# Differential scores of a two-layer encoder: two products with rows moved by transfers in place of three

## The chip, the cores and the metric

The kernel runs on one core of a Trainium2 chip. The metric is the device time of one execution, in microseconds (us). The core has a matrix engine (TensorE, PE in the profile, its weight loads PEld), VectorE (DVE), ScalarE (ACT), GpSimd (POOL) and SyncE (SP). SP issues nearly all transfers of this kernel. Results of TensorE go to eight banks of 128 x 512 fp32.

## What is computed

A trunk of two layers is applied, with the same weights, to two requests of 512 positions by 1024 features. Each layer has an attention part and a feed-forward part. The attention part has four heads of differential attention and four of latent attention. Cut to the first kind:

```
q, k = rope(h @ w_q), rope(h @ w_k)              # per head two components c of 64 features
sc   = einsum('bqhcd,bkhcd->bhcqk', q, k) * 64 ** -0.5
p    = softmax(sc)
a    = p[:, :, 0] - lam * p[:, :, 1]
o    = a @ v                                     # then rms norm, output projection, residual
```

All is fp32. The kernel splits an fp32 operand into a high part, rounded to fp32r, and a low part, the difference. A product of two operands is made as high x high + high x low + low x high, three matmuls into one bank.

## The kernel before

The program goes through layer 0 and layer 1; in each it does the attention of request 0, the attention of request 1 (the document calls these four stretches halves, numbered in order of time), and then the feed-forward part of both requests.

In a half each engine follows an order written out by hand: `TENSOR_ORDER` (L71), `SCALAR_ORDER` (L83) and `VECTOR_ORDER` (L94). Semaphores connect them; an engine that waits holds everything behind it in its order. The steps that matter here:

- TensorE: `P q0` is the projection of the two components of head 0's q to one bank (24 matmuls of 512 columns); `Pa` and `Pb` are its first and second half where it is cut in two. `S i` are the scores of unit i. Units 0 to 15 are differential: unit i is head i // 4 and a block of 128 queries, i mod 4, and has two scores, one for each component c. `T i` transposes the combined probabilities, `A` multiplies them with the values, `ST` and `RB` belong to norms.
- ScalarE: `RH` writes the high part of a roped tile (L1437, `rope_his`), `EX i` the exponentials of unit i, `TH` the high part of the transposed probabilities (L1485).
- VectorE: `RP` applies the rotary tables from the bank into the tile r1 (L1904, `rope`), `RL` makes the low part (L1920, `rope_los`), `MX` the maxima of a unit, `CB` combines the two components, `TL` makes the low part of the transposed probabilities.

TensorE begins a half's heads with `P q0 | P k0 | P q1 | S 0 | Pa k1 | S 1 | Pb k1 | T 0 | S 2 | Pa q2 | S 3 | T 1 | Pb q2 | Pa k2 | S 4`. So the first score of head 0 stands behind the projection of q1, and that of head 1 is unit 4. ScalarE has `EX 0 | EX 1 | RH q1 | TH 0 | EX 2 | TH 1 | RH k1 | EX 3 | TH 2`, VectorE `RL q1 | MX 2 | TL 0 | RP k1 | CB 2 | RL k1 | MX 3`.

A q tile has 128 rows: 32 of component 0, 32 of component 1, then the second halves of both again. `qd[n][c]` holds q's high and low part for component c: the rows of the other component are zero, since the copy multiplies with a mask (L1447, L1934). `kd[n]` holds the high and the low part of both components. n is the head mod 2, so a tile is written again two heads later. A score is the three matmuls of `product` (L526): q high by k high (L528), q high by k low (L529), q low by k high (L530), with 128 query columns as weights and 512 key columns moving. Half the rows of q add nothing to it.

The weights of a chunk (1 MB with both parts) are loaded by SP from memory as TensorE frees one of three slots (L619). In the first half ScalarE and POOL make the two parts from the raw weights (L1519, L853) and SP stores them.

Of the kernel before, what the change touches and what calls it, by code (L numbers as in the profile page):

```python
# [9 lines left out]
ACT = mybir.ActivationFunctionType  # L10
F32 = mybir.dt.float32
F32R = mybir.dt.float32r
# [3 lines left out]
P = 128  # L16
D = 1024
KT = D // P
T = 512
NT = T // P  # L20
L = 2
B = 2
H = 4
# [43 lines left out]
def order(text):  # L67
# [13 lines left out]
    ob5 | P ob6 | P ob7  # L81
""")
SCALAR_ORDER = order("""  # L83
    V | RH q0 | RH k0 | EX 0 | EX 1 | RH q1 | TH 0 | EX 2 | TH 1 | RH k1 | EX 3 | TH 2 | EX 4 | RH q2 | EX 5 | TH 3 |
    YC 0 | TH 4 | RH k2 | EX 6 | RH q3 | TH 5 | EX 7 | TH 6 | EX 8 | RH k3 | TH 7 | EX 9 | EX 10 | SH y0 | TH 8 |
    YC 1 | TH 9 | EX 11 | LC ckv | TH 10 | EX 12 | RH kpe | SH y1 | TH 11 | EX 13 | EX 14 | SH ckv | LC cq0 | LC cq1 |
    TH 12 | EX 15 | TH 13 | SH cq | YC 2 | PH kn0 | TH 14 | PH qn0 | TH 15 | RH pe0 | EX 16 | PH vm0 | PH vm1 |
    PH vm2 | YC 3 | PH vm3 | PH kn1 | SH y2 | EX 17 | TH 16 | PH qn1 | EX 18 | EX 19 | SQ 0 | PH kn2 | SQ 1 | TH 17 |
    SH y3 | EX 20 | SQ 2 | TH 18 | PH qn2 | RH pe1 | PH kn3 | EX 21 | TH 19 | PH qn3 | EX 22 | EX 23 | EX 24 | TH 20 |
    YC 4 | EX 25 | EX 26 | TH 21 | TH 22 | EX 27 | TH 23 | TH 24 | SQ 3 | SQ 4 | YC 5 | TH 25 | EX 28 | TH 26 |  # L90
    EX 29 | EX 30 | SQ 5 | SQ 6 | TH 27 | SQ 7 | SN 0 | TH 28 | SN 1 | SN 2 | TH 29 | EX 31 | SN 3 | SN 4 | SN 5 |
    TH 30 | YC 6 | TH 31 | YC 7 | SN 6 | SN 7
""")
VECTOR_ORDER = order("""  # L94
    V | RP q0 | RL q0 | RP k0 | RL k0 | RP q1 | MX 0 | MX 1 | CB 0 | CB 1 | RL q1 | MX 2 | TL 0 | RP k1 | CB 2 |
# [37 lines left out]
def numbered(names):  # L133
    return {n: i for i, n in enumerate(names)}
# [2 lines left out]

DV_MM = 7
ROPED = numbered([s[1] for s in VECTOR_ORDER if s[0] == "RP"])
ROPE_SPLITS = numbered([(n, c) for n in ROPED for c in range(2 if n[0] in "qp" else 1)])  # L140
PLAIN = numbered(["dv0", "dv1", "dv2", "dv3"] + [s[1] for s in VECTOR_ORDER if s[0] == "PL"])
LATENT = numbered([s[1] for s in SCALAR_ORDER if s[0] == "LC"])
OUTS = numbered([s[1] for s in VECTOR_ORDER if s[0] == "XO"])
# [127 lines left out]
def encoder_trunk(nc, xT, watt, wffn, tables, gains, lam, out):  # L271
    with ExitStack() as ctx:
        KB = 1024
# [7 lines left out]
        def at(name, shape, offset, dt=F32):  # L281
            return nc.alloc_sbuf_tensor_at(name, shape, dt, offset=offset)

        def psum(name):
# [53 lines left out]
        p_hi, p_lo = [ppair[:, i, :] for i in range(2)]  # L338
        qd = [[[at(f"qd{n}{c}_{s}", [P, T], r_qk + (n * 12 + c * 4 + i * 2) * KB, F32R)
                for i, s in enumerate(("hi", "lo"))] for c in range(2)] for n in range(2)]  # L340
        kd = [[at(f"kd{n}_{s}", [P, T], r_qk + (n * 12 + 8 + i * 2) * KB, F32R)
               for i, s in enumerate(("hi", "lo"))] for n in range(2)]

        cq = [[at(f"cq{n}_{s}", [P, T], r_qk + (n * 4 + i * 2) * KB, F32R)
               for i, s in enumerate(("hi", "lo"))] for n in range(2)]
# [62 lines left out]
        def sem(name):  # L408
            return ctx.enter_context(nc.semaphore(name))
# [46 lines left out]
        s_roped = Count(sem("roped"), len(ROPED))  # L456
        s_rope_hi = Count(sem("rope_hi"), len(ROPE_SPLITS))
        s_rope_lo = Count(sem("rope_lo"), len(ROPE_SPLITS))
        s_latent = Count(sem("latent_copied"), len(LATENT))
        s_xo = Count(sem("output_added"), len(OUTS))  # L460
        s_score = Count(sem("scores_done"), NEV)
# [70 lines left out]
        def stacked_product(pe, out_ap, lhs, rhs, first):  # L532

            nc.tensor.matmul(out_ap, lhs, rhs[0], start=first, stop=False)  # L534
            return nc.tensor.matmul(out_ap, lhs, rhs[1], start=False, stop=True)  # L535

        def rope_target(name):

            if name == "kpe":
                return [kpe], None  # L540
            n = int(name[-1])
            if name[0] == "p":
                return [qpe[2 * n], qpe[2 * n + 1]], 2
            return (qd[n % 2], 0) if name[0] == "q" else ([kd[n % 2]], None)

        def plain_target(name):
            n = int(name[2])
# [456 lines left out]
        def _(pe):  # L1004
# [135 lines left out]
            def scores(l, b, i):  # L1140
                h, qt = i // NT, i % NT
                at_q = slice(qt * P, (qt + 1) * P)
                for c in range(2 if i < 16 else 1):
                    ev = 2 * i + c if i < 16 else 32 + i - 16
                    dst = bank[2 + ev % 3][:]

                    pe.wait_ge(s_exp.sem, s_exp.half_at(l, b, ev - 3))
                    if ev < 3:

                        pe.wait_ge(s_plain_lo.sem, s_plain_lo.half_at(l, b, PLAIN[f"dv{ev}"]))  # L1150
                    if i < 16:
                        if qt == 0:

                            pe.wait_ge(s_rope_lo.sem, s_rope_lo.half_at(l, b, max(ROPE_SPLITS[(f"k{h}", 0)], ROPE_SPLITS[(f"q{h}", 1)])))
                        last = product(pe, dst, [qd[h % 2][c][s][:, at_q] for s in range(2)],
                                       [kd[h % 2][s][:] for s in range(2)], True, True)
                    else:
                        h -= H
                        if qt == 0:
                            pe.wait_ge(s_plain_lo.sem, s_plain_lo.half_at(l, b, max(PLAIN[f"qn{h}"], PLAIN[f"kn{h}"])))  # L1160
                            pe.wait_ge(s_rope_lo.sem, s_rope_lo.half_at(l, b, max(ROPE_SPLITS[(f"pe{h // 2}", h % 2)],
                                                                                 ROPE_SPLITS[("kpe", 0)])))
                        product(pe, dst, [qn[h % 2][s][:, at_q] for s in range(2)], [kn[h % 2][s][:] for s in range(2)],
                                True, False)
                        last = stacked_product(pe, dst, qpe[h][:, at_q], [kpe[s][:] for s in range(2)], False)
                    last.then_inc(s_score.sem, 1)
# [220 lines left out]
        def _(act):  # L1387
# [49 lines left out]
            def rope_his(l, b, name):  # L1437
                dst, scale = rope_target(name)
                act.wait_ge(s_roped.sem, s_roped.half_at(l, b, ROPED[name]))
                if name[0] == "p":  # L1440
                    act.wait_ge(s_mm.sem, s_mm.half_at(l, b, DV_MM + LAST_Z))
                elif name == "kpe":
                    act.wait_ge(s_score.sem, s_score.half_at(l, b, 23))
                elif int(name[1]) > 1:
                    act.wait_ge(s_score.sem, s_score.half_at(l, b, 8 * int(name[1]) - 9))
                for c, d in enumerate(dst):
                    nc.scalar.activation((d if name[0] == "p" else d[0])[:], r1[:], ACT.Copy, scale=1.0 if scale is None else  # L1447
                                         masks[:, scale + c:scale + c + 1]).then_inc(s_rope_hi.sem, 1)

            def latent_copy(l, b, name):  # L1450

# [90 lines left out]
            for l in range(L):  # L1542
                for b in range(B):
                    for step in SCALAR_ORDER:
                        kind, what = step[0], step[-1]
                        if l == 0 and b == 0:
                            for j in FIRST_ROUNDS.get(" ".join(str(word) for word in step), []):
                                slot_hi(j)
                        if kind == "V":
                            if b == 0:  # L1550
                                act.wait_ge(s_dg.sem, s_dg.layer_at(l, 0))
                            else:
                                act.wait_ge(s_dg.sem, s_dg.half_at(l, 0, STATS.index("n")))
                            for m in range(NT):

                                act.wait_ge(s_mm.sem, s_mm.half_at(l, b, 3 + m))
                                nc.scalar.activation(v[0][:, m, :], bank[2 + m][:], ACT.Copy,
                                                     scale=rstd[:, m:m + 1]).then_inc(s_plain_hi.sem, 1)
                        elif kind == "RH":
                            rope_his(l, b, what)  # L1560
                        elif kind == "LC":
                            latent_copy(l, b, what)
                        elif kind == "PH":
                            plain_hi(l, b, what)
                        elif kind == "EX":
                            exponentials(l, b, what)
                        elif kind == "TH":
                            transposed_hi(l, b, what)
                        elif kind == "YC":
                            head_out(l, b, what)  # L1570
                        elif kind == "SH":
                            normed_hi(l, b, what)
                        elif kind == "SQ":
                            norm_square("tail", l, b, what)
                        elif kind == "SN":
                            x_hi("tail", l, b, what)
# [226 lines left out]
        def _(dve):  # L1803
# [116 lines left out]
            def rope_los(l, b, name):  # L1920
                q0 = min(n for (tn, c), n in ROPE_SPLITS.items() if tn == name)
                dst, scale = rope_target(name)
                for c, d in enumerate(dst):
                    dve.wait_ge(s_rope_hi.sem, s_rope_hi.half_at(l, b, q0 + c))
                    if name[0] == "p":
# [554 lines left out]
```

## Time and profile before

| | |
|---|---|
| median of 3 runs | 2270.39 us (2268.04 to 2270.62) |
| profiled execution | 2269.12 us |
| its span | 2267.3 us |
| mean granted clock of TensorE | 0.997 |
| PE busy | 2232.9 us, 98% |
| DVE busy | 1803.7 us, 80% |
| ACT busy | 984.7 us, 43% |
| POOL busy | 990.3 us, 44% |
| TensorE matmuls | 10610 |

How to read it: the shares are means over the whole span, attention and feed-forward together. The granted clock is given as a share of full speed (1.00 is 2.4 GHz, 0.50 is 1.2 GHz). The duration of a matmul is longer than the distance to the next one, since matmuls overlap. The four halves lie at about 0 to 240, 240 to 490, 1115 to 1360 and 1360 to 1600 us. The profiled execution's own time is 1.8 us above its span.

### The profile page before, as it was taken

The numbers are of one execution on the slowest core, as the hardware profiler recorded it, in microseconds if no ns is written. First come the engines' busy times: TensorE is split into PE (matmuls) and PEld (weight loads), VectorE is DVE, ScalarE is ACT, GpSimd is POOL, SyncE is SP. The second block draws the span as 40 slices with busy tenths as digits, with TensorE's granted clock in tenths as the row PEclk, the third lists the DMA queues.
The fourth block names the chain that finished last, engine by engine and source line by source line (L and its number), as shares of the span: only waits on it lengthen the run. The fifth ranks groups of instructions, "written<-read, shape, count | busy, mean of one in ns | idle before, by whom it ended". The sixth has DMA issues, their size and how long they took to land.

```text
span 2267.3 us, 31231 instructions
## 1 busy us (share of the span) xinstructions
PE 2232.9 (98%) x10610; PEld 1858.7 (82%) x10610; DVE 1803.7 (80%) x2793; ACT 984.7 (43%) x1876; POOL 990.3 (44%) x686
## 2 busy tenths in 40 slices
PE   8999999999999999999999999999999999999998
PEld 6888888888888888888888888888888888888886
DVE  7998388888787878999958873988877676779988
ACT  4556144554444444443324541455444434444342
POOL 4314100124777777798700010001254455568893
PEclk9999999999999999999999999999999999999999
DMA  8633542233676766853243136312323232357522
GB/s 306 221 111 124 205 174 94 83 141 117 215 239 215 236 216 235 316 175 108 99 149 112 56 130 214 121 59 110 135 84 111 97 111 97 111 212 261 165 72 84
DMA packets 93463, 346.89 MB, mean 153 GB/s; under 512 B 9760, under 2 KB 9888, under 8 KB 74016
## 3 DMA queue, kind: packets, MB, share of 16 engines
q1 hardware_dynamic: 92624, 344.53, 43.7%
q8 instruction: 64, 1.05, 0.2%
q10 hardware_dynamic: 720, 0.86, 0.1%
q14 instruction: 55, 0.45, 0.1%
HBM read 237.35 MB, written 108.00 MB: 152 GB/s over the span
## 4 chain that ended last, share of the span: by engine, by line
PE 87%; DVE 6%; issue 1%; ACT 1%; POOL 0%; DVEq 0%; ACTq 0%; POOLq 0%
PE bank L528 28%; PE bank L530 27%; PE bank L529 27%; PE bank L1177 2%; PE bank L1015 1%; DVE x L2234 1%; DVE u L2200 1%; PE bank L1023 1%; PE bank L535 1%; PE bank L534 1%; DVE qpe L1928 1%; DVE aT_lo L2053 1%; DVE y_out L2341 0%; ACT aT_hi L1490 0%; DVE x L2242 0%
## 5 line engine op out<-in xcount | busy, mean ns | idle before, releaser
L905 POOL TENSOR_TENSOR slot<-raw,slot 128x512 fp32r<-128x512 f32 x160 | 223.4, 1400 | 234.4 <-ACT slot L1629 234.4
L528 PE MATMUL bank<-h_hi,slot 128*128 128x512 f32 x640 | 249.2, 389 | 0.0
L529 PE MATMUL bank<-h_lo,slot 128*128 128x512 f32 x640 | 249.1, 389 | 0.0
L530 PE MATMUL bank<-h_hi,slot 128*128 128x512 f32 x640 | 249.1, 389 | 0.0
L882 POOL TENSOR_TENSOR acc<-sq,zero 128x512 f32<-128x512 f32 x5 | 6.1, 1219 | 528.3 <-ACT sq L1418 528.3
L528 PE MATMUL bank<-u,slot 128*128 128x512 f32 x560 | 218.6, 390 | 1.1 <-DVE x L2234 1.1
L529 PE MATMUL bank<-u,slot 128*128 128x512 f32 x560 | 218.1, 389 | 0.0
L530 PE MATMUL bank<-u,slot 128*128 128x512 f32 x560 | 218.0, 389 | 0.0
L528 PE MATMUL bank<-h_hi,w 128*128 128x512 f32 x512 | 203.6, 398 | 0.0
L905 POOL TENSOR_TENSOR slot<-s_stage,slot 128x512 fp32r<-128x512 f32 x120 | 175.8, 1466 | 60.1 <-ACT slot L1629 58.6
L530 PE MATMUL bank<-h_hi,w 128*128 128x512 f32 x512 | 200.0, 391 | 0.0
L529 PE MATMUL bank<-h_lo,w 128*128 128x512 f32 x512 | 199.6, 390 | 0.0
L864 POOL TENSOR_TENSOR w<-raw,w 128x512 fp32r<-128x512 f32 x70 | 101.1, 1466 | 215.2 <-ACT w L1525 111.8
L529 PE MATMUL bank<-t_lo,slot 128*128 128x512 f32 x480 | 186.9, 389 | 0.0
L528 PE MATMUL bank<-t_hi,slot 128*128 128x512 f32 x480 | 186.9, 389 | 0.0
L530 PE MATMUL bank<-t_hi,slot 128*128 128x512 f32 x480 | 186.9, 389 | 0.0
L2234 DVE TENSOR_TENSOR x<-x,bank 128x512 f32<-128x512 f32 x280 | 175.3, 676 | 10.9 <-PE bank L530 10.6
L2200 DVE TENSOR_TENSOR u<-uf,u 128x512 fp32r<-128x512 f32 x140 | 170.5, 1257 | 13.8 <-ACT u L1659 13.8
L1482 ACT ACTIVATE e<-bank,mx 128x512 f32<-128x512 f32 x192 | 130.6, 686 | 99.1 <-DVE mx L2045 99.0
L2156 DVE TENSOR_TENSOR bank<-bank,snap 128x512 f32<-128x512 f32 x80 | 55.7, 696 | 143.7 <-PE bank L530 143.7
L1639 ACT ACTIVATE snap<-bank 128x512 f32<-128x512 f32 x160 | 95.5, 597 | 152.0 <-PE bank L530 151.9
L1629 ACT ACTIVATE slot<-raw 128x512 fp32r<-128x512 f32 x160 | 100.1, 627 | 97.1 <-DVE raw L2145 52.3
(261 smaller groups left out, 5931.6 us busy)
## 6 DMA issues: line engine op xcount, KB each, us to landing
w<-parked SPq DMA_DIRECT2D x81, 1024.0 KB, 4.9
raw<-in_wffn SPq DMA_DIRECT2D x112, 512.0 KB, 3.5
u_kept<-made SPq DMA_DIRECT2D x148, 256.0 KB, 2.8
uf<-u_kept SPq DMA_DIRECT2D x70, 512.0 KB, 5.7
parked<-w SPq DMA_DIRECT2D x27, 1024.0 KB, 6.3
parked<-p SPq DMA_DIRECT2D x27, 1024.0 KB, 4.9
raw<-in_watt SPq DMA_DIRECT2D x27, 512.0 KB, 4.3
praw<-in_watt SPq DMA_DIRECT2D x27, 512.0 KB, 5.8
```

The lines of the kernel that those rows point to most:

```text
L528: nc.tensor.matmul(out_ap, lhs[0], rhs[0], start=first, stop=False, skip_group_check=joins)
L529: nc.tensor.matmul(out_ap, lhs[0], rhs[1], start=False, stop=False, skip_group_check=joins)
L530: return nc.tensor.matmul(out_ap, lhs[1], rhs[0], start=False, stop=last, skip_group_check=joins)
L864: last = nc.gpsimd.tensor_tensor(w[slot][1][:, cols], src[:, cols], w[slot][0][:, cols].bitcast(F32), ALU.subtract)
L905: nc.gpsimd.tensor_tensor(slot[i][:, 1, :], gate_source(i), slot[i][:, 0, :].bitcast(F32), ALU.subtract).then_inc(s_gate_lo.sem, 1)
L1177: last = nc.tensor.transpose(bank[5][:, k * P:(k + 1) * P], src[:, k * P:(k + 1) * P], ident[:])
L1482: nc.scalar.activation(e[e_buffer(ev)][:], bank[2 + ev % 3][:], ACT.Exp, bias=mx[:, ev:ev + 1], accum_out=ls[:, ev:ev + 1]).then_inc(s_exp ...
L1629: nc.scalar.activation(slot[i][:, 0, :], gate_source(i), ACT.Copy).then_inc(s_gate_hi.sem, 1)
L1639: nc.scalar.activation(snap[n][:], bank[4 * (1 - tt) + at][:], ACT.Copy).then_inc(s_snap.sem, 1)
L2156: nc.vector.tensor_tensor(z[:], z[:], snap[2 * b][:], ALU.add).then_inc(s_joined.sem, 1)
L2200: nc.vector.tensor_tensor(upair[d % 2][g][:, q, 1, :], upair_f[d % 2][g][:, q, 1, :], upair[d % 2][g][:, q, 0, :].bitcast(F32), ALU.subtra ...
L2234: nc.vector.tensor_tensor(xn, xn, at[m][:], ALU.subtract if g == N3 else ALU.add).then_inc(s_acc.sem, 1)
```

## The change

A differential score takes two matmuls. The high part of k is written twice, into `kd[n][0]` and `kd[n][1]`; the low part of k goes to a tile of its own, `k_low`. Then small transfers issued by ScalarE put, in `kd[n][c]`, the low rows of component c in the place of the other component's rows, and, in `qd[n][c]` high, a second copy of component c's rows in the place of the zero rows. With that, one product of q high with `kd[n][c]` is high x high + high x low, and the product of q low, whose other rows are still zero, with the same tile is low x high. The step is named `MV` in ScalarE's order. It waits for the low part of its tile (q's low part reads the zero rows, k's low part is what is moved), and issues four transfers, each of 32 rows by 512 elements (64 KB). The first score of a head waits for the transfers' semaphores. `MV` stands in ScalarE's order behind `RH q0`, behind `RH k0`, between `TH 1` and `RH k1` (for q1), behind `EX 3` (k1), behind `TH 4` (q2), behind `EX 6` (k2), behind `TH 6` (q3) and behind `EX 9` (k3). The orders of the other engines are the same.

```diff
 SCALAR_ORDER = order("""
-    V | RH q0 | RH k0 | EX 0 | EX 1 | RH q1 | TH 0 | EX 2 | TH 1 | RH k1 | EX 3 | TH 2 | EX 4 | RH q2 | EX 5 | TH 3 |
+    V | RH q0 | MV q0 | RH k0 | MV k0 | EX 0 | EX 1 | RH q1 | TH 0 | EX 2 | TH 1 | MV q1 | RH k1 | EX 3 | MV k1 |
+    TH 2 | EX 4 | RH q2 | EX 5 | TH 3 | YC 0 | TH 4 | MV q2 | RH k2 | EX 6 | MV k2 | RH q3 | TH 5 | EX 7 | TH 6 |
+    MV q3 | EX 8 | RH k3 | TH 7 | EX 9 | MV k3 | EX 10 | SH y0 | TH 8 | YC 1 | TH 9 | EX 11 | LC ckv | TH 10 | EX 12 |
...
-        kd = [[at(f"kd{n}_{s}", [P, T], r_qk + (n * 12 + 8 + i * 2) * KB, F32R)
-               for i, s in enumerate(("hi", "lo"))] for n in range(2)]
+        kd = [[at(f"kd{n}{c}", [P, T], r_qk + (n * 12 + 8 + c * 2) * KB, F32R) for c in range(2)] for n in range(2)]
+        k_low = at("k_low", [P, T], r_s + 6 * KB, F32R)
...
+        s_q_moved = [sem(f"q_high_rows_doubled{n}") for n in range(2)]
+        s_k_moved = [sem(f"k_low_rows_placed{n}") for n in range(2)]
...
+        def doubled_product(pe, out_ap, lhs, rhs):
+
+            nc.tensor.matmul(out_ap, lhs[0], rhs, start=True, stop=False)
+            return nc.tensor.matmul(out_ap, lhs[1], rhs, start=False, stop=True)
...
+        def moved_value(l, b, h):
+
+            return 4 * 16 * ((l * B + b) * (H // 2) + h // 2 + 1)
+
+        def block_rows(c):
+
+            return [(own, 32 * (own // 32 ^ 1)) for own in (32 * c, 64 + 32 * c)]
...
-                            pe.wait_ge(s_rope_lo.sem, s_rope_lo.half_at(l, b, max(ROPE_SPLITS[(f"k{h}", 0)], ROPE_SPLITS[(f"q{h}", 1)])))
-                        last = product(pe, dst, [qd[h % 2][c][s][:, at_q] for s in range(2)],
-                                       [kd[h % 2][s][:] for s in range(2)], True, True)
+                            pe.wait_ge(s_q_moved[h % 2], moved_value(l, b, h))
+                            pe.wait_ge(s_k_moved[h % 2], moved_value(l, b, h))
+                        last = doubled_product(pe, dst, [qd[h % 2][c][s][:, at_q] for s in range(2)], kd[h % 2][c][:])
...
+            def move_rows(l, b, name):
+
+                n = int(name[1]) % 2
+                act.wait_ge(s_rope_lo.sem, s_rope_lo.half_at(l, b, ROPE_SPLITS[(name, 1)]))
+                for c in range(2):
+                    for own, other in block_rows(c):
+                        if name[0] == "q":
+                            tile_ = qd[n][c][0].bitcast(F32)
+                            act.dma_start(tile_[other:other + 32, :], tile_[own:own + 32, :]).then_inc(s_q_moved[n], 16)
+                        else:
+                            act.dma_start(kd[n][c].bitcast(F32)[other:other + 32, :], k_low.bitcast(F32)[own:own + 32, :]).then_inc(
+                                s_k_moved[n], 16)
...
+                if key_tile(name):
+                    h = int(name[1])
+                    dve.wait_ge(s_rope_hi.sem, s_rope_hi.half_at(l, b, q0 + 1))
+                    if h:
+                        dve.wait_ge(s_k_moved[(h - 1) % 2], moved_value(l, b, h - 1))
+                    nc.vector.tensor_tensor(k_low[:], r1[:], dst[0][:].bitcast(F32), ALU.subtract).then_inc(s_rope_lo.sem, 2)
+                    return
```

## Rows read from the trace of the kernel before

**Rows 1.** The page's busy time, share of the span and instructions.

```profile
PE 2232.9 (98%) x10610; PEld 1858.7 (82%) x10610; DVE 1803.7 (80%) x2793; ACT 984.7 (43%) x1876; POOL 990.3 (44%) x686
```

**Rows 2.** Windows: length, busy time of each engine, granted clock, DMA share, GB/s.

```profile
45.00:60.00 15.00, 14.04 (x62) 11.33 (x61) 12.70 (x21) 7.24 (x18) 5.93 (x4) 1.00 0.75 286
...
140.00:150.00 10.00, 7.77 (x54) 7.32 (x54) 8.90 (x20) 5.38 (x12) 4.52 (x4) 0.86 0.66 247
...
1404.00:1416.00 12.00, 12.00 (x55) 9.94 (x54) 8.80 (x14) 2.49 (x6) 0.00 (x0) 1.00 0.79 285
...
1432.00:1463.00 31.00, 31.00 (x169) 26.48 (x168) 28.05 (x59) 14.48 (x33) 0.00 (x0) 1.00 0.33 111
```

**Rows 3.** The tile of the low keys: duration in ns, first and last start.

```profile
L529 PE MATMUL bank<-kd_lo,qd_hi x128: 386/390/402, 52.1 to 1496.8; 128*128 128x512 f32 x128
```

**Rows 4.** Timeline of PE, fourth half: start, duration, instruction (units 0, 4, 8).

```profile
1410.96 0.39 PE L528 MATMUL bank<-kd_hi,qd_hi 128*128 128x512 f32 x1
...
1411.64 0.39 PE L528 MATMUL bank<-kd_hi,qd_hi 128*128 128x512 f32 x1
...
1430.97 0.39 PE L528 MATMUL bank<-kd_hi,qd_hi 128*128 128x512 f32 x1
...
1455.72 0.39 PE L528 MATMUL bank<-kd_hi,qd_hi 128*128 128x512 f32 x1
```

**Rows 5.** Timeline of VectorE, fourth half.

```profile
1409.24 0.69 DVE L1932 TENSOR_TENSOR kd_lo<-r,kd_hi 128x512 fp32r<-128x512 f32 x1 [0.70 <-ACT kd_hi L1447]
...
1415.92 1.37 DVE L2045 TENSOR_REDUCE mx<-bank 128x1 f32<-128x512 f32 x2 [0.74 <-PE bank L530]
...
1424.67 0.69 DVE L1918 TENSOR_TENSOR r<-r,r 128x512 f32<-128x512 f32 x1
...
1426.84 0.69 DVE L1932 TENSOR_TENSOR kd_lo<-r,kd_hi 128x512 fp32r<-128x512 f32 x1 [0.36 <-ACT kd_hi L1447]
1427.45 1.28 DVE L2045 TENSOR_REDUCE mx<-bank 128x1 f32<-128x512 f32 x2
...
1446.10 0.69 DVE L1932 TENSOR_TENSOR kd_lo<-r,kd_hi 128x512 fp32r<-128x512 f32 x1 [0.41 <-ACT kd_hi L1447]
```

**Rows 6.** Timeline of ScalarE, fourth half.

```profile
1408.57 0.63 ACT L1447 ACTIVATE kd_hi<-r 128x512 fp32r<-128x512 f32 x1 [4.10 <-DVE r L1918]
...
1425.69 0.60 ACT L1490 ACTIVATE aT_hi<-bank 128x512 fp32r<-128x512 f32 x1 [2.77 <-PE bank L1177]
1426.18 0.62 ACT L1447 ACTIVATE kd_hi<-r 128x512 fp32r<-128x512 f32 x1
...
1428.17 0.69 ACT L1482 ACTIVATE e<-bank,mx 128x512 f32<-128x512 f32 x1 [1.36 <-DVE mx L2045]
```

**Rows 7.** Timeline: DMA issues on ScalarE's queue at the kernel's start.

```profile
14.82 0.33 ACTq L1533 DMA_DIRECT2D e<-in_lam  x1
...
15.19 0.48 ACTq L1534 DMA_DIRECT2D cs<-in_tables  x1
```

**Rows 8.** The page's DMA issues: KB each, median us from issue to landing.

```profile
out_yT<-y_out SPq DMA_DIRECT2D x8, 256.0 KB, 2.2
...
g<-in_gains SPq DMA_DIRECT2D x1, 36.0 KB, 1.8
...
ident<-in_tables ACTq DMA_DIRECT2D x1, 64.0 KB, 4.8
```

**Rows 9.** Timelines of VectorE and PE at head 0, first and third half.

```profile
50.65 1.00 DVE L1932 TENSOR_TENSOR kd_lo<-r,kd_hi 128x512 fp32r<-128x512 f32 x1 [0.70 <-ACT kd_hi L1447]
...
51.80 0.47 PE L528 MATMUL bank<-kd_hi,qd_hi 128*128 128x512 f32 x1 [0.96 <-DVE kd_lo L1932]
...
1173.57 0.69 DVE L1932 TENSOR_TENSOR kd_lo<-r,kd_hi 128x512 fp32r<-128x512 f32 x1 [0.70 <-ACT kd_hi L1447]
...
1174.41 0.47 PE L528 MATMUL bank<-kd_hi,qd_hi 128*128 128x512 f32 x1
```

**Rows 10.** Timeline of PE: the wait in the window of lower clock.

```profile
145.58 0.65 PE L1023 MATMUL bank<-ident,yy 128*128 128x128 f32 x4 [2.19 <-DVE yy L1874]
```

More of the change, by code:

```diff
@@ L83 @@
 SCALAR_ORDER = order("""
-    V | RH q0 | RH k0 | EX 0 | EX 1 | RH q1 | TH 0 | EX 2 | TH 1 | RH k1 | EX 3 | TH 2 | EX 4 | RH q2 | EX 5 | TH 3 |
[L85 to L92, printed above, removed]
+    V | RH q0 | MV q0 | RH k0 | MV k0 | EX 0 | EX 1 | RH q1 | TH 0 | EX 2 | TH 1 | MV q1 | RH k1 | EX 3 | MV k1 |
+    TH 2 | EX 4 | RH q2 | EX 5 | TH 3 | YC 0 | TH 4 | MV q2 | RH k2 | EX 6 | MV k2 | RH q3 | TH 5 | EX 7 | TH 6 |
+    MV q3 | EX 8 | RH k3 | TH 7 | EX 9 | MV k3 | EX 10 | SH y0 | TH 8 | YC 1 | TH 9 | EX 11 | LC ckv | TH 10 | EX 12 |
+    RH kpe | SH y1 | TH 11 | EX 13 | EX 14 | SH ckv | LC cq0 | LC cq1 | TH 12 | EX 15 | TH 13 | SH cq | YC 2 |
+    PH kn0 | TH 14 | PH qn0 | TH 15 | RH pe0 | EX 16 | PH vm0 | PH vm1 | PH vm2 | YC 3 | PH vm3 | PH kn1 | SH y2 |
+    EX 17 | TH 16 | PH qn1 | EX 18 | EX 19 | SQ 0 | PH kn2 | SQ 1 | TH 17 | SH y3 | EX 20 | SQ 2 | TH 18 | PH qn2 |
+    RH pe1 | PH kn3 | EX 21 | TH 19 | PH qn3 | EX 22 | EX 23 | EX 24 | TH 20 | YC 4 | EX 25 | EX 26 | TH 21 | TH 22 |
+    EX 27 | TH 23 | TH 24 | SQ 3 | SQ 4 | YC 5 | TH 25 | EX 28 | TH 26 | EX 29 | EX 30 | SQ 5 | SQ 6 | TH 27 | SQ 7 |
+    SN 0 | TH 28 | SN 1 | SN 2 | TH 29 | EX 31 | SN 3 | SN 4 | SN 5 | TH 30 | YC 6 | TH 31 | YC 7 | SN 6 | SN 7
 """)
@@ L139 @@
 ROPED = numbered([s[1] for s in VECTOR_ORDER if s[0] == "RP"])
-ROPE_SPLITS = numbered([(n, c) for n in ROPED for c in range(2 if n[0] in "qp" else 1)])
+ROPE_SPLITS = numbered([(n, c) for n in ROPED for c in range(1 if n == "kpe" else 2)])
 PLAIN = numbered(["dv0", "dv1", "dv2", "dv3"] + [s[1] for s in VECTOR_ORDER if s[0] == "PL"])
@@ L543, in rope_target, with key_tile @@
                 return [qpe[2 * n], qpe[2 * n + 1]], 2
-            return (qd[n % 2], 0) if name[0] == "q" else ([kd[n % 2]], None)
+            return (qd[n % 2], 0) if name[0] == "q" else (kd[n % 2], None)
+        def key_tile(name):
+            return name[0] == "k" and name != "kpe"
+        def moved_value(l, b, h):
+            return 4 * 16 * ((l * B + b) * (H // 2) + h // 2 + 1)
+        def block_rows(c):
+            return [(own, 32 * (own // 32 ^ 1)) for own in (32 * c, 64 + 32 * c)]
         def plain_target(name):
@@ L1446, in rope_his @@
                 for c, d in enumerate(dst):
-                    nc.scalar.activation((d if name[0] == "p" else d[0])[:], r1[:], ACT.Copy, scale=1.0 if scale is None else
+                    nc.scalar.activation((d if name[0] == "p" or key_tile(name) else d[0])[:], r1[:], ACT.Copy, scale=1.0 if scale is None else
                                          masks[:, scale + c:scale + c + 1]).then_inc(s_rope_hi.sem, 1)
+            def move_rows(l, b, name):
[9 more added lines that the diff above has]
+                                s_k_moved[n], 16)
             def latent_copy(l, b, name):
@@ L1560, in _ @@
                             rope_his(l, b, what)
+                        elif kind == "MV":
+                            move_rows(l, b, what)
                         elif kind == "LC":
```

## The prediction

> **What bounds the kernel now.** I read the page's busy shares first: TensorE is busy 2232.9 of 2267.3 us [rows 1], so whatever is taken off it is worth time if nothing else becomes late. Then the table by stretches [rows 2]: in the attention stretch 1432 to 1463 us TensorE has no gap (31.00 of 31), VectorE is busy 28.05 and ScalarE 14.48. So VectorE is only 3 us behind being the bound itself. The third view is the tile of the products with the low keys [rows 3]: 128 of them, the products that go. The attention runs four times (2 layers, 2 requests; "halves" below), so 32 in each. The last views are the timelines of the three engines around the first heads [rows 4 to 6], because there the order of the work leaves the least room between a key tile's last write and its first score.
>
> **What is removed.** Three products of one score take 1411.64 - 1410.96 = 0.68 us start to start [rows 4], so one is worth 0.227 us (its 0.39 us duration overlaps its neighbour's). A unit (two scores) gets 0.454 us shorter, a half 7.26, the kernel **-29.0 us**, all of it on the engine that sets the end.
>
> **What is added.** Per head ScalarE issues four transfers for q and four for k, of 32 rows by 2 KB, 128 in all, and makes one more copy of k. VectorE's low part of k stays one instruction. The 16 more copies (0.63 us each [rows 6]) and the issues lie in ScalarE's idle half [rows 2], except where named below. VectorE's new wait before the low part of k is for the transfers of the head before, about 19 us older (1427.45 to 1446.10 [rows 5]): nothing. SP and POOL get no new step; SP's weight loads follow TensorE's progress, as before. q's transfers are issued ahead of k's and land first.
>
> Price of an issue: ScalarE's queue shows one at 14.82 and the next at 15.19 [rows 7], 0.37 us apart. No row of before has one with 32 rows, so it can be anything from nearly 0 to the 0.48 of the second one; I take 0.37. The Trainium skill, "DMA: Bandwidth & Descriptors", section "Anatomy of one DMA", states about 50 ns of sequencer dispatch for one transfer (on GpSimd's path, not this one); the rows show 0.33 and 0.48 us, and by the page the rival "cheap issue" below would hold.
>
> Price of a landing: none goes SBUF to SBUF in the trace. Small or late transfers of other kinds landed 1.8 us (36 KB) and 2.2 us (256 KB) after their issue, one of 64 KB amid loads took 4.8 [rows 8]. I take 2.0, by the two nearest in quiet, and keep 4.8 as the upper end and 1.8 as the lower.
>
> **First score of head 0.** Before, in the fourth half: k's high part 1408.57 [rows 6], its low part 1409.24 to 1409.93 [rows 5], the first score 1410.96 [rows 4], when the projection of q1 is over. So there is 1.0 us to spare. Now: one more copy (0.63), then four issues (the last starts 3 x 0.37 = 1.1 after the first), then 2.0 to land: 1409.93 + 3.73 = 1413.66, that is 2.7 us late. Second half: the same spacing, 2.7. First half: 51.65 + 3.73 against 51.80, third: 1174.26 + 3.73 against 1174.41 [rows 9], 3.6 each. Sum **+12.6 us**. Behind the waiting score on TensorE stands everything else; the next to be late is VectorE's maximum of the second unit.
>
> **First score of head 1 (unit 4).** I follow the fourth half. With the first score at 1413.66 and shorter units, the second unit ends near 1418.2 in place of 1416.4, and VectorE, which has hardly an idle moment from 1415.92 to 1425.36 [rows 5], is 1.9 us late: k1 is roped at 1427.3. ScalarE reaches its transposed copy (1425.69 before [rows 6]) at 1426.4, and now the four issues for q1 stand between it and k1's copies (1426.18 before): 1427.9. Two copies end at 1429.15, the low part at 1429.9, then the maximum and the two exponentials of unit 3 (before: 1427.45, 1428.17 and 0.68 later) come first in ScalarE's order: the issues for k1 begin at 1431.25, the last starts at 1432.35 and lands at 1434.4. Before, this score began at 1430.97 [rows 4]: 3.4 us late. TensorE alone would be there at +2.7 - 4 x 0.454 = +0.9. So 2.5 us are waited for here, in each half: **+10.0 us**.
>
> Heads 2 and 3 are covered. k2's low part ends at 1446.79 and its first score begins at 1455.72 [rows 4, 5]: 8.9 us. The new chain needs 0.6 + 1.4 (maximum and exponentials) + 1.1 + 2.0 = 5.1, and TensorE comes up to 1.8 closer. With a landing of 4.8 us it would be 0.8 us short.
>
> **VectorE and ScalarE behind TensorE.** After unit 4 VectorE is 3.4 us late and TensorE gets shorter by some 2.7 us until 1463. VectorE has 2.95 us idle in that stretch [rows 2]. What is given back lies between 0 and 2.7 per half; I take 0.75, nearer nothing because the idle time is the larger: **+3.0 us**.
>
> **The clock.** The granted clock is 1.00 (2.4 GHz) nearly everywhere. In 140 to 150 us it is 0.86, around a wait of 2.19 us of TensorE behind a run of short products [rows 2, 10]. A mean of 0.86 between the two levels means 2.8 us at 1.2 GHz, so 1.4 us of work lost. The eight new waits are longer, 2.5 to 3.6 us, but come behind dense products. Bounds: none or all eight of them, 0 to 11.2; I take four, **+5.6 us**. The Trainium skill, "TensorE: Matmul & The Clock Gate", Part 1, says that an idle TensorE falls to 1.2 GHz; the row agrees for one wait, and by the page the rival "clock at every wait" would hold.
>
> **Sum.** -29.0 + 12.6 + 10.0 + 3.0 + 5.6 = +2.2 us. The profiled execution took 2269.12 us for a span of 2267.3 (1.8 us around it), giving 2271.3; the median of the runs is 1.3 above it, so the forecast is 2270.39 + 2.2 = **2272.6 us**. A difference under 0.2% (4.5 us) is about what a measurement of this kernel can't tell from nothing.
>
> **Rivals.**
> - **Slow landing.** The transfers are small but share the DMA engines with weight loads and the store of x: the share is 0.75 at the first score of the first half and 0.79 at that of the fourth [rows 2]. If a landing takes 4.8 us at three first scores and at unit 4 of the first half, 4 x 2.8 = +11.2: 2283.8 us. For it: the row of 4.8. Against: that transfer started with the kernel's first loads. This is the case on the slower side; with the forecast at +2.2, it passes the 4.5 us of no change from about 2.6 us per landing at these four places. Chance 0.22.
> - **Cheap issue.** If an issue costs next to nothing, the first score comes 1.1 us earlier per half, and at unit 4 another 1.5 go (0.5 or more of the hold before k1, about 1.0 at the end): 4 x 2.6 = -10.4, 2262.2 us, and with fewer clock drops down to 2257. It passes -4.5 us from issues of about 0.13 us and less, which save two thirds of it. For it: in the trace the issues on ScalarE's queue run beside its copies. Against: their spacing of 0.37. Chance 0.27.
> - **Clock at every wait.** 8 x 1.4 in place of 5.6: 2278.2 us. For it: the new waits are longer than the one that cost clock. Chance 0.09.
> - **VectorE becomes the bound.** All that TensorE gains to 1463 is given back: 4 x 2.7 in place of 3.0, 2280.4 us. Against: 2.95 us idle there. Chance 0.05.
> - **It is hidden after all.** The transfers land before their scores and the change keeps its 29.0 us: 2241.4 us. Against: 1.0 us to spare at three first scores at best, less than the fastest landing of the trace. Chance 0.04.
>
> **Chances.** The forecast has 0.33. Faster by over 0.2%: most of cheap issue (0.22), all of hidden (0.04) and the forecast's lower tail (0.04), 0.30. Slower: 0.20 of slow landing, 0.06 of the clock, 0.04 of VectorE, 0.06 of the forecast, 0.36. The rest, 0.34, is within. The range, 2259 to 2286 us, reaches over cheap issue and slow landing; outside are the hidden case, and the worst meetings of two of them (every landing 4.8 us would add 22).
>
> **What would show it.** In the new profile: two score products per score, 0.227 us apart; TensorE waiting for a DMA at the first score of head 0 (about 2.7 to 3.6 us) and of head 1 (about 2.5) in each half and nowhere at heads 2 and 3; DMA issues on ScalarE's queue 0.37 us apart and landings of 2.0; windows with a granted clock under 1.00 after some waits. I am wrong if the waits at units 0 and 4 sum to under 12 or over 35 us, or if VectorE is named as releaser for more than a few us.

## The result and the profile after

The changed kernel takes **2332.91 us** (2332.12 to 2334.95, 4 runs) against 2269.22 (2267.76 to 2270.62, 4 runs) for the one before: ratio 1.0282, 95% interval 1.0264 to 1.0300. It is slower by 64 us; the forecast was 2272.6, with a range that ends at 2286. The profiled span is 2333.2 us (before 2267.3), the mean granted clock 0.980 (before 0.997).

The list of waits of TensorE, after:

```profile
engine line waited for: us in total, times, longest us
PE bank L541 <- DMA kd<-k_low: 64.3, 8, 13.4
...
PE bank L541 <- ACT e L1513: 3.5, 6, 1.4
...
PE bank L1195 <- DVE e L2046: 2.0, 4, 0.8
```

Eight waits for a transfer, 64.3 us together: the first score of head 0 and of head 1 in each half, and no others. So the places are those of the forecast, and the sum is nearly three times its 22.6 us. TensorE's timeline at four of them (the first half, then the fourth):

```profile
66.09 0.77 PE L541 MATMUL bank<-kd,qd_hi 128*128 128x512 f32 x1 [13.41 <-DMA kd<-k_low]
...
98.04 0.76 PE L541 MATMUL bank<-kd,qd_hi 128*128 128x512 f32 x1 [10.40 <-DMA kd<-k_low]
...
1473.03 0.77 PE L541 MATMUL bank<-kd,qd_hi 128*128 128x512 f32 x1 [10.70 <-DMA kd<-k_low]
1473.59 0.63 PE L542 MATMUL bank<-kd,qd_lo 128*128 128x512 f32 x1
1474.02 0.63 PE L541 MATMUL bank<-kd,qd_hi 128*128 128x512 f32 x1
...
1497.55 0.77 PE L541 MATMUL bank<-kd,qd_hi 128*128 128x512 f32 x1 [4.24 <-DMA kd<-k_low]
```

Head 0 waits 13.41, 10.56, 6.55 and 10.70 us in the four halves, head 1 10.40, 4.20, 4.22 and 4.24. Behind the wait the products start 0.43 us apart (1473.59 to 1474.02), not 0.227. Table by stretches, fourth half, after:

```profile
core 0: us, PE busy (x) PEld busy (x) DVE busy (x) ACT busy (x) POOL busy (x), PEclk, DMA share, GB/s
1462.00:1473.00 11.00, 0.32 (x2) 0.01 (x1) 2.76 (x4) 0.00 (x0) 0.00 (x0) 0.71 0.85 334
1473.00:1476.00 3.00, 2.97 (x7) 2.42 (x8) 1.38 (x2) 0.94 (x3) 0.00 (x0) 0.50 0.02 5
1476.00:1480.00 4.00, 4.00 (x17) 3.22 (x17) 0.77 (x2) 0.66 (x3) 0.00 (x0) 0.89 0.00 0
1480.00:1485.00 5.00, 5.00 (x26) 4.12 (x25) 4.86 (x11) 3.52 (x8) 0.00 (x0) 1.00 0.30 80
```

Two things stand here. While TensorE waits, the DMA engines are busy (0.85, 334 GB/s), and no transfer of 64 KB makes that. And the granted clock is 0.50 for the 3 us behind the wait, that is 1.2 GHz, and back at 1.00 (2.4 GHz) by 1480. ScalarE's timeline with its queue shows the same stretch from the other side:

```profile
1456.54 2.45 ACTq L1476 DMA_DIRECT2D qd_hi<-qd_hi  x4
1459.78 1.15 ACT L1465 ACTIVATE kd<-r 128x512 fp32r<-128x512 f32 x2 [4.10 <-DVE r L1951]
1461.76 3.53 ACTq L1478 DMA_DIRECT2D kd<-k_low  x4
...
1487.87 2.44 ACTq L1476 DMA_DIRECT2D qd_hi<-qd_hi  x4
1490.36 1.15 ACT L1465 ACTIVATE kd<-r 128x512 fp32r<-128x512 f32 x2 [1.89 <-issue]
```

Its last issue for the keys at head 0 and at head 1:

```profile
1464.24 1.05 ACTq L1478 DMA_DIRECT2D kd<-k_low  x1
...
1495.41 0.61 ACTq L1478 DMA_DIRECT2D kd<-k_low  x1
```

From there to the score it is 8.8 us at head 0 (1464.24 to 1473.03) and 2.1 at head 1 (1495.41 to 1497.55). In the halves one to four it is 7.0, 8.1, 4.2 and 8.8 us at head 0, and 7.6, 2.2, 2.1 and 2.1 at head 1. So five of the eight landings were slow, and three were near the forecast's 2.0.

Four issues take 2.44 us, 0.61 each, in the quiet case, and 3.53 at 1461.76. At 1490.36 ScalarE's own copies of k1 stand still for 1.89 us behind the issues. SyncE's timeline says what else moves then:

```profile
1457.28 0.53 SPq L656 DMA_DIRECT2D x_kept<-x  x1
1462.35 28.58 SPq L637 DMA_DIRECT2D w<-parked  x3
```

The page's list of transfers (KB each, median us from issue to landing), after, and the landing of the key transfers over all 64:

```profile
w<-parked SPq DMA_DIRECT2D x81, 1024.0 KB, 4.9
...
x_kept<-x SPq DMA_DIRECT2D x4, 2048.0 KB, 10.3
qd_hi<-qd_hi ACTq DMA_DIRECT2D x64, 64.0 KB, 2.1
kd<-k_low ACTq DMA_DIRECT2D x64, 64.0 KB, 3.5
```

```profile
DMA to landing us min/median/max: 1.9/3.5/8.6
```

In the second and the fourth half head 0's key rows are sent behind the 2 MB store of x and beside a 1 MB weight load. The fastest landing of all 64 took 1.9 us, the slowest 8.6; the times above run on to the start of the score.

### The profile page after: what moved, and what is told of

The parts are those of the page before. It is cut to its first block and busy times, and to the rows that moved or that the text cites. A ratio compares the mean times of both kernels' runs of the same rounds, so it can differ in the third digit from the quotient of the medians.

```text
span 2333.2 us, 31143 instructions
## 1 busy us (share of the span) xinstructions
PE 2230.7 (96%) x10482; PEld 1848.9 (79%) x10482; DVE 1800.8 (77%) x2793; ACT 994.1 (43%) x1892; POOL 991.0 (42%) x686
## 5 line engine op out<-in xcount | busy, mean ns | idle before, releaser
L530 PE MATMUL bank<-h_hi,w 128*128 128x512 f32 x512 | 206.7, 404 | 0.0
L532 PE MATMUL bank<-h_hi,w 128*128 128x512 f32 x512 | 202.2, 395 | 0.0
L2274 DVE TENSOR_TENSOR x<-x,bank 128x512 f32<-128x512 f32 x280 | 175.1, 675 | 10.8 <-PE bank L532 10.5
L2085 DVE TENSOR_REDUCE mx<-bank 128x1 f32<-128x512 f32 x192 | 125.7, 682 | 66.8 <-PE bank L542 61.3
```

What stands on the lines that cost most here:

```text
L530: nc.tensor.matmul(out_ap, lhs[0], rhs[0], start=first, stop=False, skip_group_check=joins)
L532: return nc.tensor.matmul(out_ap, lhs[1], rhs[0], start=False, stop=last, skip_group_check=joins)
L2085: nc.vector.tensor_reduce(mx[:, ev:ev + 1], bank[2 + ev % 3][:], AX_X, ALU.max, negate=True).then_inc(s_max.sem, 1)
L2274: nc.vector.tensor_tensor(xn, xn, at[m][:], ALU.subtract if g == N3 else ALU.add).then_inc(s_acc.sem, 1)
```

## The experiments

All times are medians; the kernel before, run beside them, took 2270.13 to 2271.22 us. Behind its heading a run is called by the first part of its label (e1).

**What two products alone are worth (e1_no_transfers).** No transfers, and neither TensorE nor VectorE waits for them; the products of q's high with k's low are left out of the scores.

```
-                            pe.wait_ge(s_q_moved[h % 2], moved_value(l, b, h))
-                            pe.wait_ge(s_k_moved[h % 2], moved_value(l, b, h))
+                            pe.wait_ge(s_rope_lo.sem, ...)
...
-                            move_rows(l, b, what)
+                            pass
```

> The changed kernel without its 128 transfers and without the waits for them; the scores leave out q high x k low. Theory A (the loss is the wait for the transfers, 64.3 us at 8 first scores, and the clock that these waits cost): all of that goes and the 29.0 us of the removed products stay, less up to 3 us where VectorE follows less quickly: 2240 to 2246 us, granted clock 0.997 as before. Rival B (VectorE is the bound once the products are gone): most of the 29 us is given back, 2255 to 2270 us, with waits of TensorE for VectorE of 15 us and more.

Measured 2252.19 us, ratio 0.9915 (0.9898 to 0.9931): 18.5 us saved, not 29, and a time between the two expectations. In its profile halves 2 to 4 each save 6.0 to 6.3 of 7.26 us, and the first is some 3 us longer, 1.1 of it ahead of its first score. There that score waits 2.16 us for the low keys, and the clock falls (run e1, table by stretches):

```profile
50.00:54.00 4.00, 1.84 (x9) 1.18 (x8) 2.74 (x3) 1.05 (x2) 2.23 (x2) 0.98 0.95 299
54.00:58.00 4.00, 4.00 (x12) 3.18 (x11) 2.84 (x5) 1.45 (x4) 0.00 (x0) 0.60 1.00 412
```

**What issuing costs (e2_transfers_to_scratch).** The same 128 transfers at the same places of ScalarE's order, but into a scratch tile; a score waits only for those of the head before, and so does ScalarE ahead of its next issues. The same products are left out.

```
-                            act.dma_start(tile_[other:other + 32, :], ...
+                            act.dma_start(scratch[0][other:other + 32, :], ...
```

> All 128 transfers are issued at the same places with the same sizes, but they land in a tile that nothing reads, and a head's scores wait for the transfers of the head before; the scores leave out q high x k low. Theory A (what costs is the wait from issue to landing): as without transfers, plus at most 1 us per half for ScalarE held by the issues of q1: 2241 to 2250 us. Rival C (the issues of 0.61 us hold ScalarE, or the transfers' load slows the weights): 2265 us or more, with TensorE waiting for ScalarE's exponentials or for weights.

Measured 2269.54 us, ratio 0.9993 (0.9984 to 1.0003): 17.3 us over e1. TensorE's waits in e2 name the cause; in e1 the first of these lines has 3.4 us:

```profile
PE bank L542 <- ACT e L1523: 14.0, 16, 1.9
...
PE bank L542 <- DVE k_low L1971: 3.5, 2, 2.8
```

The exponentials stand behind the issues on ScalarE, and the next score waits until an exponential has freed its bank: 10.6 of the 17.3 us in this line alone. TensorE's list names no transfer, so the load that the transfers put on the DMA engines isn't what it waits for. So a kernel whose transfers nobody waited for would be where before is. The other 63.4 us (2332.91 - 2269.54) come from waiting for the landings, the clock behind the waits included.

**Taking the store of x away (e3_x_store_later).** Its issue moves five weight loads later.

```
-                        if b == 1 and j == 9:
+                        if b == 1 and j == 14:
```

> The changed kernel, but SP stores the 2 MB of x five weight chunks later in the second and the fourth half, behind the first scores of head 0. Theory D (landing at the first score is long because the small transfers share the DMA engines with the store of x): these two waits fall from 10.6 and 10.7 us to about the 6.5 of the third half, where no such store runs: 2333 - 8 = 2325 us. Rival E (the weight loads or the transfers themselves make it long): both waits stay within 1 us and the time at 2333.

Measured 2338.28 us, ratio 1.0295 (1.0277 to 1.0312), not the 2325 expected. Head 0's wait in halves 2 and 4 fell from 10.56 to 6.32 and from 10.70 to 6.43, so the store did cost 4.2 us at each. But it now meets k2's transfers, at a head that never waited (TensorE's timeline of e3):

```profile
385.77 0.76 PE L541 MATMUL bank<-kd,qd_hi 128*128 128x512 f32 x1 [6.14 <-DMA kd<-k_low]
...
1526.12 0.77 PE L541 MATMUL bank<-kd,qd_hi 128*128 128x512 f32 x1 [3.82 <-DMA kd<-k_low]
```

All its waits for transfers come to 65.5 us, against 64.3 in the changed kernel: the store took its cost along, and the clock is 0.50 for 3.2 us behind each of the two new waits.

**Work ahead of the scores (e5_scores_later).** The projection of k1 goes ahead of head 0's first score, that of k2 ahead of head 1's.

```
-    V | P q0 | P k0 | P q1 | S 0 | Pa k1 | S 1 | Pb k1 | T 0 | ...
+    V | P q0 | P k0 | P q1 | Pa k1 | Pb k1 | S 0 | S 1 | T 0 | ...
```

> The changed kernel with TensorE's order alone altered: the projection of k1 stands ahead of the first score of head 0 (5.4 us more cover), and T 2, A 0 and the second half of k2's projection ahead of the first score of head 1 (about 4.5 us). Theory A: the 8 waits fall from 64 us by 5.4 and up to 4.2 per half, to about 26, and some of the lost clock comes back: 2285 to 2298 us. Rival F (VectorE and ScalarE start later with the same amount of work, so the wait only moves behind the scores): above 2315 us.

Measured 2315.98 us, ratio 1.0202 (1.0185 to 1.0219), far above the 2285 to 2298 of theory A and just above rival F's 2315. TensorE's waits:

```profile
PE bank L541 <- DMA kd<-k_low: 21.5, 5, 6.4
PE bank L1195 <- DVE e L2046: 12.6, 12, 1.9
...
PE bank L1195 <- DVE aT_lo L2093: 7.6, 7, 2.0
PE bank L541 <- ACT e L1513: 7.1, 10, 2.3
```

42.8 us of waiting for transfers went, only 16.9 us of time: VectorE and ScalarE get their first scores later and are then waited for, as rival F has it.

**Copies in place of transfers (e4_scalar_copies, and with the later scores e6_scalar_copies_scores_later).** Each transfer becomes a copy of 32 rows by ScalarE.

```
-                            act.dma_start(tile_[other:other + 32, :], ...).then_inc(s_q_moved[n], 16)
+                            nc.scalar.activation(qd[n][c][0][other:other + 32, :], ..., ACT.Copy).then_inc(s_q_moved[n], 1)
```

> The four transfers of q and of k become four copies of 32 rows on ScalarE: no landing, no DMA engine. Theory A (what costs is the landing, up to 10 us at a first score, and the clock behind it): the waits for a DMA go (64.3 us in the changed kernel), in their place TensorE waits for ScalarE at heads 0 and 1, about 2 us where the keys are last; 2262 to 2290 us. Rival C alone (what costs is ScalarE's hold of 2.4 us for each set): the copies hold it about as long (4 x 0.6), so the time stays at 2320 or above.

Measured 2301.16 us, ratio 1.0139 (1.0123 to 1.0154), between the two expectations. No landing, 31.8 us less; but eight waits for ScalarE are left, 31.3 us. In the halves one to four they are 5.42, 2.16, 3.30 and 2.16 us at head 0 and 4.6 at head 1 in all four, where I had expected about 2. A copy of 32 rows takes as long as one of 128 (ScalarE's timeline of e4, four copies in 2.58 us):

```profile
1457.92 2.58 ACT L1478 ACTIVATE kd<-k_low 32x512 fp32r<-32x512 f32 x4
```

At head 1 they wait behind k1's two copies, the maximum of unit 3 and its exponentials, as in the forecast's chain.

> The copies on ScalarE, and TensorE projects k1 ahead of head 0's first score and k2 ahead of head 1's. If the copies' 2.5 us at the first score are what is left, this covers them: 2250 to 2268 us. Rival F (projections put ahead of the scores leave VectorE and ScalarE without scores and their idle time is paid back later as waits for e and for the masked probabilities): slower than the copies in the old order, by 5 us or more.

Measured 2288.83 us, ratio 1.0088 (1.0073 to 1.0104): better than e4 by 12, where rival F had it slower, yet not the 2250 to 2268 expected. Waits for the combined probabilities, the transposes' low parts and the exponentials (11.4, 9.4, 11.0 us) have taken their place, as in e5.

**Only where there is cover (e8_transfers_heads_2_3, e9_scalar_copies_heads_2_3).** Heads 0 and 1 keep three products.

```
+                        if h < 2:
...
+                            last = product(pe, dst, ...)
+                        else:
...
+                            last = doubled_product(pe, dst, ...)
```

> Heads 0 and 1 keep three products and have no transfers; heads 2 and 3 have two products and the transfers. In the changed kernel TensorE never waited at heads 2 and 3. Theory G (the holds of ScalarE cost only where the next exponential is awaited, at heads 0 and 1): 64 products less, 14.5 us less by the spacing, 9 by what the run without transfers kept of it: 2256 to 2262 us. Rival C (the hold costs per issue, wherever it is, half of the 17 us): 2265 to 2272 us.

> As the one before, with copies of 32 rows on ScalarE in place of the transfers at heads 2 and 3. If only the hold of ScalarE matters here, 2.4 us of issues and 4 copies of about 0.6 us are the same: within 3 us of the one before. If landings still cost something at heads 2 and 3 (the store of x), this one is faster by more than 3 us; if copies also slow VectorE's or ScalarE's other work, it is slower by more than 3 us.

Measured 2265.38 us for e8 (ratio 0.9978, 0.9968 to 0.9988) and 2266.35 for e9 (0.9982, 0.9973 to 0.9991): faster than before by 4.8 and 3.8 us, and the two as good as the same, as expected if the hold alone matters. The total of e8 misses theory G's 2256 to 2262 and lies in rival C's 2265 to 2272. So the hold costs at heads 2 and 3 too. By the starts of unit 8 and of the sum of squares behind the last unit, this stretch of the fourth half takes 51.1 us in e8 (1455.56 to 1506.64), 50.5 in e1 and 53.8 before: the hold costs 0.6 us here. Another 0.4 stand between units 4 and 8 (25.16 us in e8, 24.75 before), in each of halves 2 to 4. The rest of what lacks is in the first half: from unit 0 to the same sum of squares it takes 104.1 us in e8 and 102.6 before.

**Another queue (e10_sync_issues_heads_2_3, e11_sync_issues_all_heads).** The same transfers are issued by SyncE, right behind the weight load that the head's own projection frees.

```
+            def moves(l, b, chunk):
+                if 0 <= chunk < NCH and CHUNKS[chunk] in (...):
+                    move_rows(l, b, CHUNKS[chunk])
...
                         load_parked(l, b, j)
+                        moves(l, b, j - WS_ATT)
```

> The kernel with transfers at heads 2 and 3 alone, its transfers issued on SyncE's queue in place of ScalarE's, each head's behind the weight load that its projection frees. If ScalarE's hold is what keeps that kernel (2265.4 us) from the whole saving of 64 products at 0.227 us (14.5 us): 2256 to 2262 us. Rival H (the weight loads behind the transfers come late, or the transfers land later behind a 256 KB load in the same queue, and TensorE waits for a DMA): 2266 us or more, with such waits in the list.

> The changed kernel with all its transfers on SyncE's queue. By the split so far (17 us for ScalarE's hold, 63 us for landings and the clock behind them) the hold goes and the landings stay: 2305 to 2320 us; the store of x now stands behind head 0's transfers, by which up to 8 us more can go. Rival (no hold of ScalarE but the same 0.6 us per issue on another queue, so nothing changes at the first scores): 2325 us or more.

Measured 2260.41 us for e10, ratio 0.9946 (0.9932 to 0.9960), as expected: no wait for a transfer at all, and 5.0 us under e8; and 2282.65 for e11, ratio 1.0047 (1.0031 to 1.0063). **The second is the changed kernel with nothing but the issuing queue and its order changed, and it is 50 us faster**, more than I had expected. SyncE's timeline of e11 in the fourth half with the last of the four key issues and TensorE's score behind it, TensorE's wait for transfers, and the landing of the key transfers:

```profile
1419.80 2.42 SPq L839 DMA_DIRECT2D qd_hi<-qd_hi  x4
1422.26 0.58 SPq L637 DMA_DIRECT2D w<-parked  x1
1425.02 2.41 SPq L841 DMA_DIRECT2D kd<-k_low  x4
1427.48 0.58 SPq L656 DMA_DIRECT2D x_kept<-x  x1
```

```profile
1426.84 0.59 SPq L841 DMA_DIRECT2D kd<-k_low  x1
...
1428.96 0.47 PE L541 MATMUL bank<-kd,qd_hi 128*128 128x512 f32 x1 [3.37 <-DMA kd<-k_low]
```

```profile
PE bank L541 <- DMA kd<-k_low: 27.4, 8, 9.5
```

```profile
DMA to landing us min/median/max: 1.9/2.0/5.8
```

The issues cost the same (2.41 us), but they hold nobody's exponentials, and in one queue with the large transfers they go out before the next of them: the store of x now stands behind the key rows. From the last key issue to the score it is 2.1 us here (1426.84 to 1428.96), where the changed kernel has 8.8. The median landing is 2.0 us, the forecast's figure. The eight waits fall to 27.4 us, 36.9 less: 3.38, 4.93 and 3.37 at head 0 and 1.2 to 1.3 at head 1 in halves 2 to 4 (forecast 2.7 to 3.6 and 2.5), but 9.53 and 2.42 in the first half, where loads and stores of weights alone keep the DMA engines busy (share 0.96 in 50 to 60 us of e11).

**The rest of the gain (e12_sync_issues_heads_1_to_3, e13_sync_issues_half_projection_first).** e12 gives head 1 its two products too. e13 is e11 with the first half of k1's projection (Pa k1) ahead of unit 0.

> Head 0 alone keeps three products; heads 1, 2 and 3 have two, their transfers on SyncE's queue. Against the kernel with heads 2 and 3 (2260.4 us) a half gains up to 3.6 us (16 products); in the kernel with all heads on SyncE's queue head 1's first score still waited 1.2 to 1.3 us in three halves, and here TensorE comes later to it, so the wait should be 1 us or less and the clock mostly kept: 2248 to 2256 us. Rival (any wait of TensorE at head 1, however short, brings the clock down for some us and gives the gain back): 2258 us or more.

> All heads in two products, transfers on SyncE's queue, and the first half of k1's projection (2.7 us) moved ahead of head 0's first score, behind which it stood. It covers 2.7 of the 3.4 to 4.9 us that head 0's first score waits in halves 2 to 4. If the wait and the clock behind it are what is left (four waits, 11 us of them and 6 of clock), the kernel comes from 2282.7 to 2262 to 2272 us. Rival F (what stands ahead of the scores is paid back as waits for the exponentials and the masked probabilities): 2278 us or more.

Measured 2259.46 us for e12, ratio 0.9954 (0.9941 to 0.9968), not to be told from e10. That is above the 2248 to 2256 expected and in the rival's range. My expectation priced head 1 wrongly: it has 8 products a half, 1.8 us, not 16. By the starts of units 4 and 8 (1423.82 to 1446.86 against 24.76 us in e10) 1.7 of these came, and the wait took 1.0 back. The rival's reason doesn't hold all the same, since the clock stays up behind this wait (e12's table by stretches and timeline):

```profile
1423.80:1427.00 3.20, 3.18 (x22) 2.93 (x23) 2.68 (x6) 1.54 (x4) 0.00 (x0) 1.00 0.81 310
```

```profile
1423.82 0.47 PE L541 MATMUL bank<-kd,qd_hi 128*128 128x512 f32 x1 [1.02 <-DMA kd<-k_low]
```

Measured 2271.20 us for e13, ratio 1.0004 (0.9995 to 1.0013): 11.5 us under e11, within its 2262 to 2272, and level with before. The waits for transfers fell from 27.4 to 16.6 us, and all of that came through. One small piece of work moved ahead is paid back less than a whole projection.

**The first half** is a case of its own. In e10, the stretch from unit 8 to unit 14 in the first half and in the fourth:

```profile
98.50:133.90 35.40, 33.91 (x182) 27.76 (x180) 34.09 (x77) 20.92 (x49) 8.77 (x6) 1.00 0.56 188
1450.50:1483.60 33.10, 33.10 (x181) 28.06 (x180) 29.63 (x72) 16.47 (x39) 0.00 (x0) 1.00 0.35 112
```

VectorE, the fourth number, is busy 34.09 of 35.4 us (96%) there and 29.63 of 33.1 in the fourth half. Part of that is that some of its instructions take longer in this stretch: those that combine the components 894 ns in place of 752, the low part of q 1265 in place of 746. GpSimd is busy there (8.77 us) and idle in the fourth half; whether that is the reason no run shows. From unit 8 to the sum of squares behind the last unit e10 takes 57.37 us in the first half, before 57.35: nothing comes of the shorter scores. In the fourth it takes 50.44 against 53.81, 3.4 of the 3.6 us.

## Why the prediction was wrong

- **The places were right.** Waits at heads 0 and 1 in each half, none at heads 2 and 3, no new work on VectorE. By the forecast's own sign (waits of over 35 us at units 0 and 4) it is wrong: they sum to 64.3.
- **The landing is the step that failed.** "I take 2.0, by the two nearest in quiet" was read from quiet rows, and the transfers are sent beside loads. In the fourth half the low keys end at 1461.72, the issues begin at 1461.76, the last of them starts at 1464.24, and the score starts at 1473.03: 8.8 us from the last issue to the score, above the upper end of 4.8. All four at head 0 and that of head 1 in the first half were slow (4.2 to 8.8 us); over 2.0 each, the eight landings make 26 of the 41.7 us by which the waits exceed the forecast's 22.6. The rival "slow landing" had the mechanism and sized it with the 4.8 us at four places only. That row belonged to the kernel's first loads; the share of 0.79 in [rows 2] at the first score was the warning. The rows have no line of SyncE's queue, where the 2 MB store goes out 2.5 us ahead of k's high part (before, SyncE's timeline):

```profile
1406.08 0.43 SPq L638 DMA_DIRECT2D x_kept<-x  x1
```

- **The price of an issue** was 0.61 us, not 0.37, above the upper end of 0.48. From the first key issue to the last it takes 1.8 to 1.9 us in place of 1.1 in the quiet case, and 3.7, 3.1 and 2.5 at head 0 of the first, second and fourth half, beside the large transfers. That is 10 more of the 41.7 us. In halves 2 to 4 head 1's landing was as forecast (2.1 to 2.2 us), and the 1.7 us that its wait is longer than the 2.5 forecast are those of the issues: 0.9 us more for q1's four, 0.7 to 0.8 for k1's.
- **The hold of ScalarE was missing.** It was priced only at k1's copies, as part of the wait at unit 4. e2 against e1 shows 17.3 us over the kernel, and e8 against e10 5.0 us for half of the issues. ScalarE idles half of the stretch [rows 2], but its idle time doesn't lie where the issues stand: those of q1 stand ahead of k1's copies and of unit 3's exponentials, 2.44 us, of which ScalarE waited 1.89.
- **The clock.** All eight waits brought it down, not four. From unit 0 to unit 1 it takes 5.84, 6.54, 6.30 and 5.54 us where the rows of before less 0.45 give 3.6 to 3.7, from unit 4 to 5 4.4 in place of 2.8: together some 16 us, not 5.6. Other waits lie between: the clock fell behind 2.16 us (e1) and in [rows 10], and held behind 1.02 (e12). The new waits were far longer than the 2.5 to 3.6 us that the term was made for.
- **What the 29.0 us were worth.** Without any transfer 18.5 came. The forecast took 3.0 for what VectorE gives back; the first half alone gave back its whole 7.26, and e10 shows its own 3.6 given back there with VectorE 96% busy. So the rival "VectorE becomes the bound" fits one half of four; that VectorE is the cause there is read from its share and not from a run that relieves it.
- **The sum of the profiled run:** -29.0 + 64.3 + 16 leaves 14.6 to the 65.9 us by which the span grew. Nearly all of that is saving that e1 lacks too: its span is 15.8 us under before (2251.5), 13.2 short of the 29.0. So the hold's 17.3 us, seen where no landing is waited for, hide here for the most part behind the landings; the two don't add up, and no run separates them within the changed kernel.
- **The chances.** 0.36 stood on slower, but no case reached 2286. Landings slow at many places were counted among "the worst meetings" and left out, though they have one cause, the large transfers on SyncE's queue. Even every landing at 4.8 us would have added only 22.

The Trainium skill, "DMA: Bandwidth & Descriptors", section "Issuing engines are not separate DMA queues", says that issuing from another engine saves only the issue time on the sequencer, and that this is usually small beside the transfer. Here it isn't small (2.41 to 2.45 us for four, of which e2 shows 17.3 us in the time), and e11 gained 50 us, with the queue and the order changed together: the sentence leaves out what the order between small and large transfers is worth. What of the 50 is order and what is the hold isn't split by a run; if the hold were its whole 17.3 us, 33 would remain for the order.

## What to carry to other kernels

A small transfer between two dependent steps costs what the queues beside it carry at that moment: read the DMA share and the large transfers issued just ahead, and where landings share one cause, put them at the slow end together. Issue it on the queue that carries the large transfers and ahead of the next of them, not on the queue of an engine whose results are awaited. Use it only where the consumer comes late enough: of the 16 units of a half, the eight with 8 us of cover gave 10.8 of their 14.5 us (2260.41 us, 0.54% under before), and the eight without it gave all or nearly all of theirs back, or more, in every order tried.

## What was not expected

- The issue of a 32-row transfer took 0.51 us as the first of a row and 0.59 to 0.65 behind another, on ScalarE's queue and on SyncE's alike, and up to 1.74 beside large transfers (first half of the changed kernel).
- The 64 KB of a key transfer landed in 1.9 to 8.6 us from ScalarE's queue (median 3.5) and in 1.9 to 5.8 (median 2.0) from SyncE's in e11, with the same loads in another order.
- A copy of 32 by 512 on ScalarE took 0.63 us, as one of 128 by 512 does.
- A wait of TensorE of 1.02 us left the granted clock at 1.00, one of 2.16 us in e1 was followed by 0.60 over 4 us. But e12's wait of 2.18 us at head 1 of the first half was followed by a clock of 1.00 and a unit 4 of 2.88 us. In e4 head 0 waits 2.16 us in the second half and in the fourth, behind the same work at a clock of 1.00, and the clock falls once and holds once (table by stretches, from the score on). Why, no run here shows.

```profile
308.80:312.00 3.20, 3.18 (x9) 2.57 (x10) 2.07 (x3) 1.50 (x4) 0.00 (x0) 0.62 0.94 399
1437.60:1440.80 3.20, 3.20 (x14) 2.65 (x15) 1.98 (x3) 1.45 (x4) 0.00 (x0) 1.00 0.95 407
```

- The first score of the first half came between 51.5 and 54.4 us in kernels whose work up to it is the same (e8, e10, e12), and the clock in 20 to 40 us was 0.91 in e8, 1.00 before. So a gain under 3 us can't be read from one profile of the first half.
